# Projections moved between the attention, bonus and retention products, another launch order and another order in the second block

## The reference

```python
for l in range(DEPTH):                       # DEPTH = 2
    h = rms_norm(x, ln_mix_pre[l])
    z = h @ w_in[l]                          # 1024 -> 7436 columns
    z_q, z_kv, z_g, z_ret, z_rwkv, z_conv, z_gate = split_cols(z, IN_SIZES)
    o_nsa = nsa_mixer(...)                   # compressed, selected, windowed attention
    o_ret = retention_mixer(r_q, r_k, r_v, r_g, ret_norm_g[l])
    o_rwkv = rwkv7_mixer(z_rwkv, ...)        # recurrence, head norm, plus a "bonus" term
    o_conv = short_conv_mixer(z_conv, conv_w[l])
    gates = jax.nn.sigmoid(z_gate).reshape(B, S, N_BRANCHES, D_MODEL)
    merged = sum of gates[:, :, m] * (branches[m] @ w_branch[l, m])
    # output projection, norm, residual; cross-attention to mem; MLP of width 4096
```

## Time and profile before

| what | before |
|---|---|
| time, median of 3 runs | 2109.21 us (2103.8 to 2111.39) |
| time of the profiled execution | 2104.69 us |
| its span | 2102.9 us, 30304 instructions |
| PE busy | 1915.1 us (91%) |
| DVE, ACT busy | 1426.7 us (68%), 1168.5 us (56%) |
| chain that ended last | PE 65%, DVE 22%, ACT 8% |
| mean granted TensorE clock | 0.961 of full |

### The profile page before, as it was taken

The page is one execution under the profiler, slowest core; times in us unless marked ns, Lnnn a source line. Parts: engine busy times, 40 slices in busy tenths (PEclk is TensorE's granted clock), DMA queues, the critical chain, the costliest instruction groups (busy, mean ns, idle before and its releaser), DMA issues.

```text
span 2102.9 us, 30304 instructions
## 1 busy us (share of the span) xinstructions
PE 1915.1 (91%) x12946; PEld 1747.3 (83%) x12946; DVE 1426.7 (68%) x1425; ACT 1168.5 (56%) x1310; POOL 76.5 (4%) x94
## 2 busy tenths in 40 slices
PE   4999997988999889997997999897779999999997
PEld 3989997987998889997997999796668888888885
DVE  3686547545555677637645555755679999999995
ACT  2644344544444554333644444454368888888884
POOL 0000013000000000013000000000000000000000
PEclk9999998998999999999998999998879999999998
DMA  7333374524554333356542555332259999999993
GB/s 265 127 141 136 119 266 162 200 101 142 193 189 159 156 141 131 127 178 243 186 159 105 190 195 181 134 121 86 94 224 374 375 375 380 377 379 374 375 391 135
DMA packets 64524, 440.87 MB, mean 210 GB/s; under 512 B 7372, under 2 KB 7372, under 8 KB 14592
## 3 DMA queue, kind: packets, MB, share of 16 engines
q1 hardware_dynamic: 55296, 399.63, 50.6%
q0 software_dynamic: 8096, 35.30, 4.5%
q10 hardware_dynamic: 992, 3.93, 0.5%
HBM read 428.61 MB, written 10.23 MB: 209 GB/s over the span
## 4 chain that ended last, share of the span: by engine, by line
PE 65%; DVE 22%; ACT 8%; issue 2%; POOL 1%; DMA 1%; DVEq 0%; ACTq 0%; POOLq 0%
PE psum L188 64%; DVE ring_low L202 6%; ACT hl L198 3%; DVE arena L212 3%; DVE ht L202 2%; DVE rounded L202 2%; DVE rounded L212 2%; DVE arena L202 2%; ACT arena L198 1%; PE psum L192 1%; POOL arena L202 1%; DVE hl L202 1%; ACT rounded L198 1%; DVE arena L225 1%; DVE resid L202 1%
## 5 line engine op out<-in xcount | busy, mean ns | idle before, releaser
L202 DVE TENSOR_TENSOR hl<-ring,hl 128x2048 fp32r<-128x2048 f32 (+1 forms) x190 | 433.9, 2286 | 350.7 <-ACT hl L198 350.3
L188 PE MATMUL psum<-ht,hl 128*128 128x256 f32 x4992 | 630.2, 288 | 15.4 <-DVE hl L202 9.7
L188 PEld LDWEIGHTS psum<-ht,hl 128*128 128x128 f32 x4992 | 616.2, 195 | 25.1 <-DVE hl L202 10.3
L198 ACT ACTIVATE hl<-ring 128x2048 fp32r<-128x2048 f32 (+1 forms) x286 | 536.3, 1896 | 150.7 <-PE psum L188 122.9
L188 PE MATMUL psum<-hl,ax 128*128 128x512 f32 (+1 forms) x1608 | 351.9, 355 | 6.4 <-DVE ax L202 5.0
L198 ACT ACTIVATE arena<-psum 128x512 f32<-128x512 f32 (+5 forms) x232 | 121.0, 522 | 418.5 <-PE psum L188 405.5
L188 PEld LDWEIGHTS psum<-hl,ax 128*128 128x128 f32 x1608 | 264.8, 192 | 47.3 <-DVE ax L202 5.3
L202 DVE TENSOR_TENSOR ring_low<-ring,hl 128x2048 fp32r<-128x2048 f32 x96 | 215.3, 2285 | 19.3 <-ACT hl L198 19.1
L188 PE MATMUL psum<-arena 128*128 128x128 f32 (+6 forms) x1520 | 190.8, 291 | 30.1 <-ACT arena L198 23.5
L188 PEld LDWEIGHTS psum<-arena 128*128 128x128 f32 (+2 forms) x1520 | 174.7, 179 | 41.6 <-ACT arena L198 25.2
L188 PE MATMUL psum<-hl,ht 128*128 128x256 f32 (+1 forms) x1056 | 132.2, 287 | 26.8 <-DVE ht L212 24.0
(11 more groups left out here) (121 smaller groups left out, 1897.7 us busy)
## 6 DMA issues: line engine op xcount, KB each, us to landing
ring<-W SPq DMA_DIRECT2D x284, 1024.0 KB, 5.1
arena<-W SPq DMA_DIRECT2D x48, 1024.0 KB, 7.5
ht_raw<-W SPq DMA_DIRECT2D x46, 1024.0 KB, 7.8
gate_d<-arena POOLq DMA_DIRECT2D x32, 256.0 KB, 3.8
arena<-gate_d POOLq DMA_DIRECT2D x8, 1024.0 KB, 8.0
gn<-GB POOLq DMA_DIRECT2D x10, 512.0 KB, 4.1
arena<-GB POOLq DMA_DIRECT2D x6, 512.0 KB, 4.9
ring<-W SPq DMA_DIRECT2D x4, 512.0 KB, 4.5
```

The costliest lines, as they stand in the source:

```text
L188: return Nothing() if self.e is None else self.e.matmul(o, a, b, start=start, stop=stop, skip_group_check=skip_group_check)
L198: return self.e.activation(o, a, f, bias=bias, scale=scale)
L202: return Nothing() if self.e is None else self.e.tensor_tensor(o, a, b, op)
```

## The change

It touches three places.

Launch: x is loaded first. Each engine waits for x alone before the norm, and for the other three loads behind it. GpSimd asks for the gain row without a wait. The cuts of the first three units and the projection `kcks` stand ahead of the bias matrix and of the wait for `bias_d`.

Layers: one filler moves from behind the attention's output product to ahead of it, and one from behind the retention's variance to ahead of the bonus sum. ScalarE and VectorE each cut one unit ahead of taking the attention's output, and VectorE cuts none between the LoRA's input norm and its `lor` step. The number of fillers is the same.

Second block: the four `unit()` move behind the gelu on ScalarE and behind the last `log_weight` on VectorE. `1 - a^2` was formed from t = tanh(log a) as 2t / (t - 1), with a reciprocal and of the sign that the root wants; now it is (a^2 + 1) t, with the sign turned in the root's scale.

```diff
@@ tensor, launch
             pe.wait_ge(s_const, 16)
-            pe.wait_ge(s_par, 16)
-            pe.wait_ge(s_x, 16)
-            pe.wait_ge(s_once, 16)
-            b = bank("rowb")
-            mm(psum[0:4, b, :], [(R("rel")[0:32, :], m0.onehot[0:32, :])]).then_inc(s_pe, P("rowb"))
             for l in range(2):
+                if l == 0:
+                    pe.wait_ge(s_par, 16)
+                    pe.wait_ge(s_once, 16)
+                    b = bank("rowb")
+                    mm(...).then_inc(s_pe, P("rowb"))
                 norm(L.nmix.xn, "mix", l)
                 if l == 0:
+                    pe.wait_ge(s_dve, V["mix", l])
+                    proj(hTv, "kcks", l)
                     pe.wait_ge(s_hank, 32)
                     for h in range(4):
...
@@ tensor, layers
                 turn_p(2)
+                fill()
                 for j in range(2):
                     b = bank("onsa", j, l)
...
-                fill(3)
+                fill(2)
                 pe.wait_ge(s_dve, V["lor", l])
...
+                fill()
                 pe.wait_ge(s_dve, V["rkr", l])
                 stats(L.t1, "bonus", l)
                 fill()
...
                 stats(L.rsqb, "rvar", l)
-                fill()
                 fill()
@@ scalar, launch
+            ac.dma_start(Xv, x_in.rearrange("b (t p) d -> p (b t) d", t=2)).then_inc(s_x, 16)
             ac.dma_start(cst[:, :], CS).then_inc(s_const, 16)
             ac.dma_start(par[:, :], PR).then_inc(s_par, 16)
-            ac.dma_start(Xv, x_in.rearrange("b (t p) d -> p (b t) d", t=2)).then_inc(s_x, 16)
             ac.dma_start(arena[:, 0:896], CO[:, 0:896]).then_inc(s_once, 16)
...
                     for t in range(2):
                         norm(Xv, L.nmix, t, "mix", l)
+                    upper()
+                    ...
                     for t in range(2):
                         norm_cut(hTv, t, "mix", l)
+                    for _ in range(LOOK):
+                        upper()
                     ac.wait_ge(s_bias, 16)
@@ scalar, second block
-            for _ in range(4):
-                unit()
             for nm, dst, o in (("wa", t1, 0), ("wx", t2, 2)):
...
-            act(t1, t1, ACT.Sqrt, "ustd")
+            act(t1, t1, ACT.Sqrt, "ustd", scale=-1.0)
             ac.wait_ge(s_dve, V["gelu"])
             act(t3, t3, ACT.Tanh, "gelu", scale=math.sqrt(2.0 / math.pi))
+            for _ in range(4):
+                unit()
             weights(3)
@@ vector, second block
-            for _ in range(4):
-                unit()
...
-            ts(t1, t3, -1.0, None, ADD, None)
-            rec(t1, t1)
-            stt(t1, t3, 2.0, t1, MUL, MUL, "uvar")
+            tt(t1, aL, aL, MUL)
+            stt(t1, t1, 1.0, t3, ADD, MUL, "uvar")
...
             log_weight(3)
+            for _ in range(4):
+                unit()
             ve.wait_ge(s_act, A["ya", 2])
```

More of the change, by code:

```diff
@@ L675, in tensor @@
             pe.wait_ge(s_const, 16)
-            pe.wait_ge(s_par, 16)
-            pe.wait_ge(s_x, 16)
-            pe.wait_ge(s_once, 16)
-            b = bank("rowb")
-            mm(psum[0:4, b, :], [(R("rel")[0:32, :], m0.onehot[0:32, :])]).then_inc(s_pe, P("rowb"))
             for l in range(2):
                 L = layers[l]
+                if l == 0:
+                    pe.wait_ge(s_par, 16)
+                    pe.wait_ge(s_once, 16)
+                    b = bank("rowb")
+                    mm(psum[0:4, b, :], [(R("rel")[0:32, :], m0.onehot[0:32, :])]).then_inc(s_pe, P("rowb"))
                 norm(L.nmix.xn, "mix", l)
                 if l == 0:
+                    pe.wait_ge(s_dve, V["mix", l])
+                    proj(hTv, "kcks", l)
                     pe.wait_ge(s_hank, 32)
@@ L690, in tensor @@
                 fill = filler(l)
-                pe.wait_ge(s_dve, V["mix", l])
-                proj(hTv, "kcks", l)
+                if l:
+                    pe.wait_ge(s_dve, V["mix", l])
+                    proj(hTv, "kcks", l)
                 proj(hTv, "q", l)
@@ L1354, in inverse_root @@
                 act(o, o, ACT.Exp, *name, scale=-0.5)
+            ac.dma_start(Xv, x_in.rearrange("b (t p) d -> p (b t) d", t=2)).then_inc(s_x, 16)
             ac.dma_start(cst[:, :], CS).then_inc(s_const, 16)
             ac.dma_start(par[:, :], PR).then_inc(s_par, 16)
-            ac.dma_start(Xv, x_in.rearrange("b (t p) d -> p (b t) d", t=2)).then_inc(s_x, 16)
             ac.dma_start(arena[:, 0:896], CO[:, 0:896]).then_inc(s_once, 16)
-            ac.wait_ge(s_const, 16)
-            ac.wait_ge(s_par, 16)
             ac.wait_ge(s_x, 16)
-            ac.wait_ge(s_once, 16)
-            ac.wait_ge(s_pe, P["rowb"])
-            copy(m0.rowb[0:4, :], psum[0:4, banks["rowb",], :], "rowb")
-            gone("rowb")
             for l in range(2):
@@ L1371, in scalar @@
                         norm(Xv, L.nmix, t, "mix", l)
+                    upper()
+                    ac.wait_ge(s_const, 16)
+                    ac.wait_ge(s_par, 16)
+                    ac.wait_ge(s_once, 16)
+                    ac.wait_ge(s_pe, P["rowb"])
+                    copy(m0.rowb[0:4, :], psum[0:4, banks["rowb",], :], "rowb")
+                    gone("rowb")
                     for t in range(2):
                         norm_cut(hTv, t, "mix", l)
-                if l == 0:
+                    for _ in range(LOOK):
+                        upper()
                     ac.wait_ge(s_bias, 16)
@@ L1997, in wide @@
                 return ap.broadcast_to([128, ap.shape[1], n])
-            ve.wait_ge(s_const, 16)
-            ve.wait_ge(s_par, 16)
             ve.wait_ge(s_x, 16)
-            ve.wait_ge(s_once, 16)
             for l in range(2):
@@ L2007, in vector @@
                         norm(Xv, L.nmix, t, "mix", l)
+                    lower_part()
+                    ve.wait_ge(s_const, 16)
+                    ve.wait_ge(s_par, 16)
+                    ve.wait_ge(s_once, 16)
                     for t in range(2):
                         norm_cut(hTv, t, "mix", l)
+                    for _ in range(LOOK):
+                        lower_part()
                     for h in range(4):
```

4 lines of the change are left out of this document (removed).

## The result

| | before | after |
|---|---|---|
| median of 4 runs beside each other | 2108.58 us | 2078.22 us |
| lowest to highest | 2103.8 to 2111.39 | 2074.36 to 2083.98 |
| profiled execution, its span | 2104.69, 2102.9 | 2074.36, 2072.6 |
| granted clock of it, mean | 0.961 | 0.964 |

The ratio is 0.9861, interval 0.9828 to 0.9894: 30.4 us less between the medians, 30.3 between the spans of the two profiles. The forecast was 2070 (2068.1 for an execution like the profiled one, 2072.6 from the median), its range 2056 to 2086. The time lies in that range and in the forecast's own (2062 to 2080), and 8 us above the forecast. The four runs of after are spread over 9.6 us, the two lowest at a granted clock of 0.964, the others at 0.961 and 0.959.

A forecast was written before the change was run, and what follows sets the result against it. Taken as bound by TensorE's chain, with gains only where it stands idle. Launch 15.0, layers 8.4 and second block 13.2 sum to 36.6 us: 2068.1 profiled, 2072.6 from the median, predicted 2070; range 2056 to 2086, forecast's own 2062 to 2080.

The forecast's parts named there:

- Launch, 15.0 forecast: Launch: x first and projection ahead of bias products bring the compression product to 46.4; gain 15.0 us, bounds 6 and 17.
- tightest place, 0.7 us: Launch, fourth projection: unit 3 cut by 40.4, needed at 41.1; any later delay adds one for one.
- The half-rate first projection: Launch: by the skill's page the first projection costs up to 6 us more and the stage gives 9.
- Two layers, 8.4 forecast: Both layers: moved fillers close TensorE's waits, part lost inside the M products; 4.2 us kept per layer, 8.4 for both.
- The step put at nothing: Layers, behind the M products: a projection between any two recurrence steps keeps TensorE's lead, so no loss was counted.
- The rival price beside it: Layers: if the new 3.6 us gap costs a clock loss too, they give 5 instead of 8.4 us.
- Second block, 13.2 forecast: Second block: the four tanh no longer wait for a weight; centring starts 13.2 us earlier, bounds 8 and 15.
- The further 1.38 of drain: Second block: by the skill's page each table switch costs another 1.38 us; three loads cost 4, the block gives 9.
- A: Layers' lead lost at the M banks and by a clock dip, launch gives 9: 24 us in all, 2083; chance 0.17.
- B: Earlier cuts wait for weight slots, one 4.7 us landing in each of three places: 14 us lost, 2086; chance 0.11.
- C: TensorE at half clock from first projection to end of first attention: 65 us added, 2133; chance 0.03.
- D: The sixth M product doesn't wait, layers give 16, and the launch gives 17: 2058; chance 0.09.

The follow-up runs named there:

- m_filler: The full change, with one filler per layer moved from behind the M products to between the transposes and the M products: 2068.51 us, ratio to before 0.9821.
- both_extra: The full change with the extra steps of m_filler and unit3_early together: 2066.85 us, ratio to before 0.9803.
- unit3_early: The full change, with weight unit 3 also cut ahead of the wait for `bias_d`: 2074.61 us, ratio to before 0.9847.
- x_third: The full change with the launch loads issued in the old order, x third: 2081.36 us, ratio to before 0.9874.
- layers_only: The kernel before with only the hunks inside the two layers: 2105.87 us, ratio to before 0.9985.

## Why the prediction came out, point by point

**Launch, 15.0 forecast, 14.5 measured: right in sum, by errors that cancel.** x landed at 10.15 instead of 9.2, and the first projection started at 22.06 instead of 21.3. The transfer of the bias matrix took 5.5 us, from 31.60 to ScalarE's next start at 37.12, instead of the 3.6 of rows 2 (31.40 to 34.96). The DMA engines are full ahead of it now, where they had little to do: slots of the ring come free earlier, and a weight unit is still loading when the transfer is asked for. The view by stretches of before (DMA share and GB/s are the last two):

```profile
26.00:31.00 5.00, 4.49 (x8) 2.23 (x8) 3.04 (x6) 0.35 (x1) 0.00 (x0) 1.00 0.27 99
31.00:35.00 4.00, 0.00 (x0) 0.00 (x0) 0.10 (x1) 0.04 (x1) 0.54 (x1) 0.74 0.48 197
```

Of after:

```profile
26.00:31.00 5.00, 5.00 (x31) 3.94 (x30) 1.99 (x5) 0.00 (x0) 0.00 (x0) 1.00 0.99 382
31.00:37.00 6.00, 6.00 (x53) 6.00 (x52) 0.30 (x1) 0.00 (x0) 0.54 (x1) 1.00 0.62 254
```

`m_filler` bears the cause out. Its engines were just as full from 26 to 31 (1.02), but that load was over when the transfer was asked for (a share of 0.04 from 33 to 34), and the transfer took 3.5; in `both_extra`, asked for at the same time, the engines stayed busy (0.92, 1.08 and 0.86 in the three microseconds behind) and it took 5.5.

With that the "tightest place, 0.7 us" gave way: unit 3 ended the wait of its projection, 2.06 us. This was named as a sign that the forecast would be wrong, and it came about. Its low part was ready at 41.3 instead of 40.4. On the other side TensorE was ready for it at 39.3 instead of 41.1, since the bias products took 2.74 instead of 4.63. That both errors met within 0.2 us of the forecast start is luck. `unit3_early` confirms the place: without its wait, the stage is 2.5 shorter.

**The clock at launch.** The prediction read 1.00 off rows 3 for the start of the program, "with little work", as the opposite of the rule of the Trainium skill ("TensorE: Matmul & The Clock Gate", Part 1), that the array is throttled until activity releases it. That reading was wrong, for before and for after. The packed traces hold their first clock record at 29.5 us in before, 20.7 in after and 25.6 in `m_filler`, and the views show 1.00 for all that lies ahead of it. The products show half rate there. In before the bias products start 0.64 us apart from 26.66 to 29.22 and 0.32 apart behind it, with one clock column of 1.00 over both. In `m_filler` 9 products of the first projection fall between 22 and 24 us, in after 16, again with 1.00 in both columns. So the array ran at the lower of its two levels, 1.2 GHz, at the start, and rose to 2.4 GHz only when TensorE had been at work: in after it works from 14.70 on and the first record stands at 20.7. By the page's rule too it starts throttled and is released by activity, and the trace agrees. In after that came ahead of the first projection, which ran at full clock (6.01); in `m_filler` and `both_extra` it came 3.6 us into it and cost 1.6 us (7.60 and 7.62). The half-rate first projection by which this stage would have given 9 instead of 15 did not occur in after, and the forecast's 4.6 us for the bias products was a half-rate price. In `x_third` the record itself falls to 0.50, from 24.9 to 28.3, and the projection takes 7.27.

**Two layers, 8.4 forecast, 7.9 measured in their own stages, 3.8 in the median of the layers alone: the term that was mis-sized.** The mechanism is the one forecast: a new wait for ScalarE's copy inside the M products (2.92, forecast 3.6), the first copy 2.3 earlier than the launch alone makes it (16.8 less 14.5; forecast 2.5). What the sum lacked is what the clock takes later. The step put at nothing, "from there TensorE has a projection between any two steps, so a lead is kept", holds for the waits and not for the clock. The loss is small in the next stretch (0.9 over the profiles) and 3.5 us in the one behind layer 1, so 4.6 of the layers' 9.0 are left. The rival price beside it was 5 for the layers, worked out from rows 4 for the case that the new gap costs a return to full clock. The rule that it went by is the Trainium skill's ("TensorE: Matmul & The Clock Gate", "HAM oscillation — how this bites in real kernels"), that the array is throttled again in a gap and pays behind it. The 3.8 of `layers_only` lies near that price, but mostly by other gaps: the new one cost nothing in both layers of after (2.94 for the 24 products behind it) and 1.6 in three of eight layers.

**Second block, 13.2 forecast, 13.2 measured at the centring step, 12.3 at the output projection.** Tanh, scores, mask, scan and low parts moved as worked out. The 0.9 between is lost behind the centring step, at four products that took 2.08 in after:

```profile
1454.97 2.08 PE L188 MATMUL psum<-arena,cst 128*128 128x256 f32 x4 [1.93 <-DVE arena L202]
```

And 1.13 behind the same wait in before:

```profile
1485.49 1.13 PE L188 MATMUL psum<-arena,cst 128*128 128x256 f32 x4 [1.93 <-DVE arena L202]
```

The twelve products from 1440.23 on ran slow too (4.54 against 2.87), but the wait behind them shrank from 6.04 to 4.48, and only 0.1 of that came through.

The table loads cost what their rows say: the one at 1426.99 lasts 1.28 and the next activation starts at 1428.29. The further 1.38 of drain of the Trainium skill ("ScalarE: Activation LUTs", What ACT_TABLE_LOAD costs), by which, as an estimate, the three loads of this chain would have left 9 of the 13, did not occur.

**The rivals.** A (the fillers give nothing, 2083) is refuted for the layers' own stages; of the whole it has the loss by the clock right, which took about half of their gain. B (the wait moves to the weights, 2086) came about nowhere: the two units of the second block are cut without a wait (1428.83), the wait ahead of the attention's output is gone, and unit 3 was late because its cut stands behind the wait for `bias_d` (13.57 us in ScalarE's row at 37.12), not for want of a filled slot. C (half clock through the first attention, 2133) did not happen: half rate ended at 20.7 us. D (more) shows in `m_filler`: what it needs is that the wait in the M products goes, and the diff has nothing that takes it away.

**The size.** From the profiled execution the forecast was 2068.1 and the time 2074.4: 6.3 too low. Launch is 0.5 of that, the layers 0.5, the block 0.9, and 4.4 the stretches between, which the sum had at nothing.

## What to carry to other kernels

Independent work put ahead of a wait gives back what it fills only as far as the engines behind the wait are early too: follow their chain to the next place where they meet (here a PSUM bank) and count the smaller lead. Such a move can be worth nothing alone and something with its neighbour, since every instruction that it displaces carries a chain of its own; try them together before giving one up. When an edit is worth a few microseconds and the kernel's runs differ by nine, read it at a mark right behind its stage, in the profiles of several kernels that share the stage, and the clock beside it. Check a clock column against the time of a product whose full-rate time is known from elsewhere in the trace.

## What the runs showed of the hardware that was not expected

- The same load landed after 10.2 us in third place, 9.4 in first, and 11.8 in third place with the gain row asked for beside it; the constants went from 7.9 to 11.4 when moved from first to second. The last load was in at 12.95 before and at 14.5 after, where the 512 KB of the gain row are among them.
- The transfer of the bias matrix to memory (768 KB) took 5.5 us where a load of a weight unit was still in flight when it was asked for (after, `both_extra`), and 3.5 where none was (before, `m_filler`). No run was built to take the weight loads alone away.
- The clock is granted or not behind the same waits of 2 to 3 us from one profile to the next: 7.14 or 8.83 for 32 products, 2.94 or 4.58 for 24.
- The granted clock reads 1.00 ahead of the first clock record (at 20 to 30 us here) though products run at half rate: 0.64 us apart instead of 0.32 in before. The first 48 products of the program took 6.01 where the clock rose ahead of them and 7.60 where it rose 3.6 us into them.
- The mean clock of a run goes with its time: 2105.4 us at 0.962, 2114.2 at 0.955 in the first job. It leaves a part open: at 0.960 the 24 runs of before in the last job lie between 2103.8 and 2109.1.
